# Projections of layers 0 and 1 as three split products with VectorE's low parts two chunks ahead, and two VectorE chains moved or cut up

## The reference

```
proj = h @ w_in                      # 256 x 1024 by 1024 x 3656
mq, mk, mv, dq, dk, dv, qi, ki, wi = split(proj)
score = sum_h(wi_h * relu(qi_h . ki / 8))      # indexer, causal
keep the 64 best keys of each query (of those not later than it)
o = [softmax attention(mq, mk, mv), the same on the kept keys (dq, dk, dv)]
```

## Time and profile before

| what | value |
|---|---|
| median of 3 runs | 2729.18 us (2726.37 to 2730.58) |
| the profiled execution's own time | 2728.39 us |
| its span, first to last instruction | 2726.5 us |
| TensorE busy | 2559.7 us, 94% of the span |
| VectorE busy | 1749.1 us, 64% |
| ScalarE busy | 1256.4 us, 46% |
| GpSimd busy | 678.8 us, 25% |
| mean granted TensorE clock | 0.96 of full |
| HBM read | 691.10 MB, 254 GB/s over the span |

### The profile page before, as it was taken

The page is one execution under the profiler, slowest core; times in us unless marked ns, Lnnn a source line. Parts: engine busy times, 40 slices in busy tenths (PEclk is TensorE's granted clock), DMA queues, the critical chain, the costliest instruction groups (busy, mean ns, idle before and its releaser), DMA issues. The chain is left out here.

```text
span 2726.5 us, 36635 instructions
## 1 busy us (share of the span) xinstructions
PE 2559.7 (94%) x14374; PEld 2079.0 (76%) x14374; DVE 1749.1 (64%) x1998; ACT 1256.4 (46%) x1300; POOL 678.8 (25%) x353
## 2 busy tenths in 40 slices
PE   7998999998999987999897699999999999999996
PEld 4874998874998764999765588888887878788884
DVE  1254666444866674755674677777777777777785
ACT  1123443223443122333112367767766767676673
POOL 0000000001920533920270122222322323232223
PEclk9998999999999988999997799999999999999997
DMA  9886764466785564865431299999999999999992
GB/s 339 278 276 203 249 209 158 147 201 215 241 238 165 169 217 133 275 212 184 140 108 47 99 367 330 366 330 369 328 367 328 351 347 347 347 346 353 337 358 104
DMA packets 434953, 693.80 MB, mean 254 GB/s; under 512 B 37691, under 2 KB 255895, under 8 KB 434839
## 3 DMA queue, kind: packets, MB, share of 16 engines
q1 hardware_dynamic: 407632, 677.17, 72.2%
q10 hardware_dynamic: 27206, 15.03, 2.0%
HBM read 691.10 MB, written 1.05 MB: 254 GB/s over the span
## 5 line engine op out<-in xcount | busy, mean ns | idle before, releaser
L1376 ACT ACTIVATE region_part<-ring 128x2048 fp32r<-128x2048 f32 x432 | 804.5, 1907 | 299.1 <-PE bank L792 200.4
L792 PE MATMUL bank<-ring_part,region_part 128*128 128x512 f32 x1648 | 649.2, 394 | 0.0
L2211 DVE TENSOR_TENSOR ring_part<-ring,region_part 128x2048 fp32r<-128x2048 f32 x270 | 640.4, 2405 | 2.8 <-ACT region_part L1376 2.8
L790 PE MATMUL bank<-region_part 128*128 128x512 f32 x1432 | 582.8, 407 | 6.2 <-DVE ring_part L2211 6.2
L791 PE MATMUL bank<-region_part 128*128 128x512 f32 x1296 | 512.1, 395 | 0.0
L1268 POOL TENSOR_TENSOR ring_part<-ring,region_part 128x2048 fp32r<-128x2048 f32 x54 | 268.4, 4979 | 554.7 <-ACT region_part L1376 554.7
L792 PEld LDWEIGHTS bank<-ring_part,region_part 128*128 128x128 f32 x1648 | 309.9, 188 | 71.5
L790 PE MATMUL bank<-xn_part,region_part 128*128 128x256 f32 x1152 | 327.4, 284 | 9.8 <-DVE hT_part L1931 9.1
L790 PEld LDWEIGHTS bank<-region_part 128*128 128x128 f32 x1432 | 269.7, 188 | 75.6 <-issue 14.6
L792 PE MATMUL bank<-hT_part,region_part 128*128 128x256 f32 x1152 | 325.9, 283 | 0.0
L791 PE MATMUL bank<-xn_part,ring_part 128*128 128x256 f32 x1152 | 325.7, 283 | 0.0
(11 more groups left out here) (295 smaller groups left out, 3412.9 us busy)
## 6 DMA issues: line engine op xcount, KB each, us to landing
ring<-in_moe_w_gate SPq DMA_DIRECT2D x126, 1024.0 KB, 5.1
ring<-in_moe_w_up SPq DMA_DIRECT2D x126, 1024.0 KB, 5.2
ring<-in_moe_w_down SPq DMA_DIRECT2D x126, 1024.0 KB, 5.0
ring<-in_w_ada SPq DMA_DIRECT2D x48, 1024.0 KB, 7.8
ring<-in_mod_w SPq DMA_DIRECT2D x48, 1024.0 KB, 5.9
ring<-in_w_in SPq DMA_DIRECT2D x44, 1024.0 KB, 5.7
ring<-in_w_up_act SPq DMA_DIRECT2D x22, 1024.0 KB, 5.4
ring<-in_w_up_lin SPq DMA_DIRECT2D x22, 1024.0 KB, 6.1
```

Of the source, the lines that this page charges most:

```text
L790: nc.tensor.matmul(o, split(a_hi), split(b_hi), start=start, stop=False, skip_group_check=True)
L792: return nc.tensor.matmul(o, split(a_hi), split(b_lo), start=False, stop=stop, skip_group_check=True)
L1376: return nc.scalar.activation(out_, in_, func, **kw).then_inc(*done(*event))
L2211: v.tensor_tensor(split(w), w, whole(hi), ALU.subtract).then_inc(*done("moe_lo", j, e))
```

## The change

Projection chunks c3 to c14 of layers 0 and 1 are multiplied by `product`, three reduced-precision products in place of one full. c0 to c2 stay as they are. ScalarE writes the high part of chunk i + 2 ahead of its `in_out` of chunk i, into one of three buffers; the third is the memory of the feed-forward's `hf` and `ffn_tmp`. VectorE writes its low part at the same place i of its own program. ScalarE writes the high part of `hT` in four pieces ahead of c0's `in_out`; VectorE writes the low part over `hT` in four pieces once TensorE has finished c2, and TensorE waits for all four ahead of c3.

The indexer's products and sums are cut in three parts, behind c6, c7 and c8, and within a part the products of two units alternate. The eight rounds of the selection stand two by two behind c9, c10, c11 and c12, and the mask is made after c14 (`key_mask`). The S5 parameters are worked out in layer 0's feed-forward: VectorE's chain in halves behind groups 1, 3, 4 and 7, ScalarE's exponentials and sines behind groups 0, 2 and 5. A table of constants is staged in other memory. `s5_params` is otherwise the same text in two branches.

```diff
+IN_WHOLE = 3
+IDX_PAIRS = [((0, 0), (0, 1)), ((1, 0), (1, 1)), ((1, 2), (1, 3))]
...
+    ffn_rows = sb_split("ffn_rows", 8 * S)
+    hf = ffn_rows[:, 0:4 * S].rearrange("p (b s) -> p b s", b=4)
+    ffn_tmp = ffn_rows[:, 4 * S:8 * S].rearrange("p (b s) -> p b s", b=4)
...
+    ci = Carve(in_at)
+    in_hi = [ci("", n=SLOT), ci("", n=SLOT), ffn_rows]
...
+            def in_tokens_split(l, n):
+                key = ("in", l, n)
+                if n == PROJ_ORDER[IN_WHOLE]:
+                    for b in range(4):
+                        pe.wait_ge(*until("hT_lo", l, "in", b))
+                pe.wait_ge(*until("w_lo", "in", l, n))
+                wh, w = in_part(l, n)
+                o = bank(key, ("in_out", l, n)).rearrange("p (t n) -> p t n", t=NT)
+                for t in range(NT):
+                    ts = slice(t * P, (t + 1) * P)
+                    for k in range(KD):
+                        m = product(o[:, t, :], hT_hi[:, k, ts], hT[:, k, ts], wh[:, k, :], w[:, k, :], k == 0, k == KD - 1)
+                m.then_inc(*done("pe_tile", *key))
...
                     for i, n in enumerate(PROJ_ORDER):
-                        if l == 0 or i >= 2:
+                        if i >= IN_WHOLE:
+                            in_tokens_split(l, n)
+                        elif l == 0 or i >= 2:
                             in_tokens(l, n)
...
-                        if i == 6:
-                            indexer_logits(l)
+                        if 6 <= i < 9:
+                            indexer_logits(l, i - 6)
...
+            def in_leading(l, i):
+                n = PROJ_ORDER[i]
+                act.wait_ge(*loaded(("in", l, n)))
+                if i >= IN_WHOLE + len(in_hi):
+                    act.wait_ge(*until("pe_tile", "in", l, PROJ_ORDER[i - len(in_hi)]))
+                hi, w = in_part(l, n)
+                run(split(hi), w, ACT.Copy, "w_hi", "in", l, n)
...
-                if l == 1:
-                    s5_params()
+                for b in range(4):
+                    run(split(hT_hi[:, 2 * b:2 * b + 2, :]), hT[:, 2 * b:2 * b + 2, :], ACT.Copy, "hT_hi", l, "in", b)
                 for i, n in enumerate(PROJ_ORDER):
+                    if IN_WHOLE <= i + 2 < len(PROJ_ORDER):
+                        in_leading(l, i + 2)
                     in_out(l, n)
...
+                    if l == 0 and g == 0:
+                        s5_steps()
+                    if l == 0 and g in (2, 5):
+                        s5_angles(2 + g // 3)
...
+            def in_low(l, n):
+                dve.wait_ge(*until("w_hi", "in", l, n))
+                hi, w = in_part(l, n)
+                v.tensor_tensor(split(w), w, whole(hi), ALU.subtract).then_inc(*done("w_lo", "in", l, n))
...
+                    if l == 0 and 1 <= g <= 7 and g != 5:
+                        half = {1: (2, 0), 3: (2, 1), 4: (3, 0), 7: (3, 1)}
+                        if g in half:
+                            s5_params(*half[g])
...
                 if l == 1:
-                    s5_params(2)
-                    s5_params(3)
                     v.tensor_copy(c_wide[:, :, AT], c_act[:, 1, :]).then_inc(*done("c_second"))
                 if l < 2:
                     for i, n in enumerate(PROJ_ORDER):
+                        if i == IN_WHOLE - 1:
+                            dve.wait_ge(*until("pe_tile", "in", l, n))
+                            for b in range(4):
+                                dve.wait_ge(*until("hT_hi", l, "in", b))
+                                h = hT[:, 2 * b:2 * b + 2, :]
+                                v.tensor_tensor(split(h), h, whole(hT_hi[:, 2 * b:2 * b + 2, :]), ALU.subtract).then_inc(*done("hT_lo", l, "in", b))
+                        if IN_WHOLE <= i + 2 < len(PROJ_ORDER):
+                            in_low(l, PROJ_ORDER[i + 2])
...
                         if i == 6:
                             dve.wait_ge(*until("in_out", l, 3))
                             rope(l, 0, 16, "rope", l, 0)
-                            indexer_sum(l)
+                        if 6 <= i < 9:
+                            indexer_sum(l, i - 6)
                         if i == 10:
                             dve.wait_ge(*until("in_out", l, 9))
                             rope(l, 1536, 16, "rope", l, 1)
-                            top_keys(l)
+                        if 9 <= i < 13:
+                            top_keys(l, (2 * (i - 9), 2 * (i - 9) + 1))
+                    key_mask(l)
```

More of the change, by code:

```diff
@@ L1486, in mixer_one @@
                         run(kiT, p_[:, 0:S], ACT.Copy, "kiT_out", l)
[L1487 to L1495, removed]
+                    if 6 <= i < 9:
+                        for t, n2 in IDX_PAIRS[i - 6]:
+                            p_ = tile("idx", l, t, n2)
+                            order = n2 + (2 if t else 0)
+                            if order >= 2:
+                                act.wait_ge(*until("idx_sum", l, order - 2))
+                            run(idx_r[:, order % 2, :], p_, ACT.Relu, "idx_relu", l, t, n2, scale=0.125)
                 for b, name in ((1, "mq"), (2, "mk")):
@@ L1957, in rope, with indexer_sum @@
                     v.tensor_tensor(y2, tc, td, ALU.add).then_inc(*(done(*event) if t else link()))
-            def indexer_sum(l):
-                order = 0
-                for t in range(NT):
+            def in_low(l, n):
+                dve.wait_ge(*until("w_hi", "in", l, n))
+                hi, w = in_part(l, n)
+                v.tensor_tensor(split(w), w, whole(hi), ALU.subtract).then_inc(*done("w_lo", "in", l, n))
+            def indexer_sum(l, part):
+                for t, n in IDX_PAIRS[part]:
+                    order = n + (2 if t else 0)
@@ L1963, in indexer_sum @@
                     kn = (t + 1) * P
                     acc = idx_acc[:, t, 0:kn]
[L1965 to L1979, removed]
+                    dve.wait_ge(*until("idx_relu", l, t, n))
@@ new lines, in indexer_sum @@
+                    heads = unit_heads(t, n)
+                    for i, h in enumerate(heads):
+                        r = idx_r[:, order % 2, i * kn:(i + 1) * kn]
+                        after()
+                        ev = done("idx_sum", l, order) if i == len(heads) - 1 else link()
+                        if (n, i) == (0, 0):
+                            v.tensor_scalar(acc, r, w_idx[:, t, h:h + 1], None, ALU.mult).then_inc(*ev)
+                        else:
+                            v.scalar_tensor_tensor(acc, r, w_idx[:, t, h:h + 1], acc, ALU.mult, ALU.add).then_inc(*ev)
@@ L1980, in indexer_sum, with top_keys @@
+                if part != 1:
+                    after()
                     v.tensor_tensor(idx_work[:, t, 0:kn], acc, causal[:, t, 0:kn], ALU.add).then_inc(*link())
-            def top_keys(l):
-                for r in range(TOPK // 8):
+            def top_keys(l, rounds):
+                for r in rounds:
                     for t in range(NT):
```

157 lines of the change are left out of this document (84 added, 73 removed).

## The result

The changed kernel takes **2712.72 us** at the median of four runs (2711.79 to 2714.05), the kernel before beside it 2729.88 (four runs, 2726.37 to 2731.44). The ratio is **0.9939, interval 0.9923 to 0.9955**: faster by 0.6%, 17.2 us where 26.6 were forecast.

A forecast was written before the change was run, and what follows sets the result against it. TensorE was taken to pace the projections and layer 0's feed-forward. The sum was 2728.39 - 30.2 + 4.6 - 1.0 = 2701.8 us for the profiled execution; the median, 0.8 above, was forecast at 2702.6, range 2697 to 2713.

The forecast's parts named there:

- The products: c3 to c14, both layers: a chunk falls from 6.92 to 5.66 us, saving 30.2 us over 24 chunks.
- Rival 4: Full products cost four passes against three reduced: chunk of 5.19 us, 41.5 us saved, 2691 us; chance 0.02.
- The split of hT, layer 1: Ahead of layer 1's c3, TensorE waits for VectorE's four low pieces of hT: +2.8 us.
- The split of hT, layer 0: Ahead of layer 0's c3, the same wait, partly covered by 1.0 us of `ada`: +1.8 us.
- rival 3: Layer 0's projections become bound by transfers: 6 us if held to 300 GB/s, 2709 us; chance 0.06.
- rival 1: TensorE's clock falls in the new stalls ahead of c3: +1.7 us each, 2704 to 2706 us; chance 0.2.
- The margins of the low parts: Low parts of the weights are ready before their chunks start, c13 and c14 by 2.4 us in layer 1: +0.
- Rival 2: VectorE is late at c13 and c14, perhaps elsewhere: 3 to 10 us, 2706 to 2713 us; chance 0.12.
- The indexer in three parts: Indexer products cut in three with two units alternating may overlap more: -1.0 us for both layers.
- The parameters moved: S5 chain, 20.1 us of VectorE in layer 1, moved into idle time of layer 0's feed-forward: +0.
- rival 5: The S5 pieces lie open in layer 0's feed-forward: TensorE waits for all 32 us, 2735 us; chance 0.03.

The follow-up runs named there:

- experiment 5: The kernel of experiment 2 with layer 0's gate bias and row loads issued behind c6 instead of ahead of c0: 2696.01 us.
- experiment 6: The changed kernel with only layer 0's gate bias and row loads issued behind c6 instead of ahead of c0: 2708.77 us.
- experiment 1: The changed kernel with products that nobody reads filling TensorE's idle time ahead of c3 in both layers: 2705.16 us.
- experiment 2: The changed kernel with hT's low part written to other, free memory at the start of the projections, not waiting for c2: 2698.00 us, 2697.64 when run again.
- experiment 7: The changed kernel with the eight rounds of the selection in one piece behind the second rope: 2729.66 us.
- experiment 3: The changed kernel with the S5 parameters worked out in layer 1's mixer again, before VectorE's other work there: 2720.67 us.
- experiment 8: The changed kernel with the high and low parts of the weights made one chunk ahead instead of two: 2719.37 us.
- experiment 4: The changed kernel with layer 0's projections left as full float32 products, only layer 1 in products of three: 2720.04 us.

## Why the prediction came out as it did

- **The products, -30.2.** Right in kind, slightly large. Six chunks of layer 1, c9 to c14, run from 529.41 to 563.82, 5.735 us each where I had 5.66. Within a chunk a triple takes 0.355 us, not the 0.351 of the earlier trace rows, and the edge is 0.05. Twenty-four chunks save 28.4. Rival 4's chunk of 5.19 us did not appear, and the rows say why the ratio stays above its 0.75: at 2.4 GHz a full product of 256 columns takes 0.432 us, 4.05 cycles a column, and a reduced one 0.355 / 3 = 0.118 us, 1.11 a column. The full product costs four; it is the reduced one that costs more than one. What its extra tenth is was not tried.
- **The split of hT, layer 1, +2.8.** Right: 2.90.
- **The split of hT, layer 0, +1.8. This step failed.** It measured 4.33, 2.5 more. I had VectorE free to run the four pieces when c2 ends; but one low part of weights stands ahead of them in its queue, and c3's weights landed at 58.6. Before the change TensorE first wanted those weights at 60.49, and that was in time. Two chunks of look-ahead move the deadline forward, and by how much a transfer is early was the one margin that I did not work out for c3, while I did for c9 to c14. The row was there: a DMA share of 1.09 in c0 to c2, which I read as "not a ceiling" in rival 3, instead of as "everything lands late". Experiments 5 and 6 show it: with 1.57 MB fewer on ScalarE's queue the stall is 1.90 us.
- **The clock, given as rival 1 with 0.2. This step failed too, and is the larger.** I left it out of the sum because the work there is dense. It fell in both stalls and cost 2.2 and 2.7 us, 4.9 where the sum had none and the rival 1.7 each. Experiments 1 and 2 show cause and size, and the wait behind four dense chunks in experiment 7 shows that dense work does not protect. The row that I had, 2.52 us of idling and half clock behind it, pointed the right way. It is no rule all the same: in experiment 2 the clock stayed at 1.00 behind 2.79 and 2.47 us.
- **The margins of the low parts, +0.** Right: TensorE waits for none from c4 to c14. Low part of c13 done 2.3 us early in layer 1 (2.4 worked out); experiment 7 hit 7.8 by the same list. For layer 0 the prediction has only the sentence that the margins grow; no low part was late there either. Rival 2 is out.
- **The indexer in three parts, -1.0.** Too large: three parts of 1.06 us (528.35 to 529.41 is one) are 3.2 a layer against 3.37, so -0.3 for both. The overlap I hoped for isn't there.
- **The parameters moved, +0, and rival 5.** Right: 200.0 us for the feed-forward either way, experiment 3.
- **Rival 3, transfers as the pace of layer 0.** Out as priced: the stage moves 296 GB/s, and 319 in experiment 5 at clock 1.00. (Its price was a slip as well: 274 / 300 of 102.55 us is 93.7, 5 us above 88.7 and not 6.) The transfers cost time at the start only, by the late landing of c3's weights.
- **Elsewhere.** +0.7 in c0 to c2 and +0.3 and -2.0 and +2.3 in stages whose TensorE work is the same, net 1.3. In the main these are spells of half clock of another length: c0 has 4.7 us of it instead of 3.4, layer 1's out-projection 10.2 instead of 3.4 (its stage takes 100.7 us instead of 98.8, 1.9 of the 2.3) and layer 0's 3.4 instead of 10.2 (the -2.0). That the last two cancel is luck, as no run shows that they belong together.
- **The range.** 2712.7 lies at the very end of 2697 to 2713, and its upper end came from rivals 2 and 3, which did not happen. That the number falls inside is no merit of the sum.

The sum again, with what was measured: 2728.4 - 28.4 + 7.2 (stalls) - 0.3 + 4.9 (clock) + 1.3 = 2713.1, against 2712.5 for the profiled execution; 0.6 us are rounding and small terms that nothing here divides up.

## What to carry to other kernels

When operands must be prepared earlier, follow the whole chain back to the transfer and work out each margin anew, for the first use above all, where the queues are full. When a change puts an idle stretch of two to five microseconds in front of dense TensorE work, count the half clock behind it as likely (it followed 16 of the 18 stretches of 1.90 us and more that the edits brought ahead of products of three, and neither of the two of 1.15 and 1.19) and as a large part of the price (4.9 us beside 7.2 of idling). Then look for memory that lets the preparation move ahead of the stretch: here a buffer that was free anyway gave 14.7 us more, 9.3 of them traced to stalls and clock. And a list of the engines' times written out by hand from the rows predicted the wait at c13 to 0.1 us, the one ahead of layer 1's c3 to 0.1 and those of experiment 8 to between 0.2 and 1.6; read starts and ends in it with care.

## What was not expected of the hardware

The granted clock does not follow the length of one idle stretch: 1.90 us (experiment 6) was followed by half clock and 2.79 us (experiment 2) was not. It isn't what ends the stall either: the low part of weights ends it in experiment 2, without a fall, and in experiment 8 (3.99 us), with one. The fall can come in the stall (2.4 us before c3 in the changed kernel) or up to 1.5 us after the products have begun again (experiment 4, c3 from 496.4 and the fall at 497.9). What tells experiment 2 apart for the clock stays open. Layer 1's out-projection, which no kernel here edits, has a spell of 10.2 us in all seven traces in which TensorE fell to half clock ahead of layer 1's c3 (the changed kernel twice, experiments 3, 4, 6, 7 and 8), and one of 3.4 us in the five others (the kernel before, experiments 1, 5 and 2 twice). If that is no coincidence, the stall in layer 1 cost another 2 us some 130 us later (the stage takes 100.7 to 101.1 us with the long spell and 98.2 to 98.8 with the short one); by what it would be passed on is open, and was not tried. Layer 0's out-projection warns against trusting it: the same two lengths stand there, 10.2 us in the kernel before and experiments 1 and 7, 3.4 us in the nine other traces, and whether the clock had fallen at layer 0's c3 does not sort them. A triple of reduced products takes 0.355 us in the projections and 0.351 in the feed-forward; this 1% was not tried apart.
